# Retention on Trainium2: the product of values and decayed scores taken as three passes of rounded halves

## The reference

```python
def _retention(h, w_in, w_out):
    proj = h @ w_in
    q, k, v, g = jnp.split(proj, [RET_QK_W, 2 * RET_QK_W, 2 * RET_QK_W + RET_V_W], axis=-1)
    k = k * RET_QK_DIM ** -0.5
    ...
    def step(state, inp):
        q_i, k_i, v_i = inp
        scores = jnp.einsum('bhid,bhjd->bhij', q_i, k_i) * intra
        o = jnp.einsum('bhij,bhje->bhie', scores, v_i) \
            + jnp.einsum('bhid,bhde->bhie', q_i * q_dec, state)
        ...
    o = _rms_norm(o).reshape(B, L, RET_V_W).astype(h.dtype)
    y = jax.nn.silu(g) * o
    return y @ w_out
```

## Time and profile before

| | us |
|---|---|
| median of 3 runs | 1148.59 |
| lowest and highest run | 1146.23, 1149.07 |
| the profiled execution | 1149.55 |
| its span in the trace | 1147.7 |
| stretch of scores and products in it | 830.8 to 862.3 |

### The profile page before, as it was taken

One profiled execution on the slowest core, in us unless ns is written; L12 is line 12 of the kernel. 1 busy time (PEld: TensorE's weight loads), 2 busy tenths in 40 slices (PEclk: granted clock), 3 DMA queues, 4 the chain that ended last, 5 costly groups with the idle time before them and its releaser, 6 DMA issues.

```text
span 1147.7 us, 24128 instructions
## 1 busy us (share of the span) xinstructions
PE 1113.4 (97%) x8921; PEld 1061.7 (93%) x8921; DVE 777.3 (68%) x1404; ACT 624.1 (54%) x1194; POOL 338.4 (29%) x372
## 2 busy tenths in 40 slices
PE   6999999999989999999999999999999999999997
PEld 5976999999989888779999999999979999999996
DVE  5776489887478767737888554695456567887454
ACT  4656575556455656655656443474335555665443
POOL 3011414334301100126666321100023344665120
PEclk8999999999999999969999999999999999999998
DMA  6564337775556623214555545564513555555651
GB/s 197 131 178 146 92 107 208 193 199 164 188 173 194 211 74 111 75 37 148 182 158 173 184 161 197 198 194 156 170 48 111 187 179 184 183 183 190 205 180 48
DMA packets 202667, 180.63 MB, mean 157 GB/s; under 512 B 6849, under 2 KB 200804, under 8 KB 202468
## 3 DMA queue, kind: packets, MB, share of 16 engines
q1 hardware_dynamic: 201907, 175.74, 49.3%
q0 software_dynamic: 688, 3.94, 0.9%
HBM read 176.28 MB, written 1.05 MB: 155 GB/s over the span
## 4 chain that ended last, share of the span: by engine, by line
PE 86%; DVE 4%; ACT 4%; issue 2%; DMA 2%; POOL 1%; SPq 0%; ACTq 0%; DVEq 0%; POOLq 0%
PE ps L1942 25%; PE ps L1944 24%; PE ps L1943 24%; PE ps L2358 2%; DVE wlo L1314 2%; PE ps L2488 2%; PE ps L2100 1%; ACT whi L769 1%; POOL acc L590 1%; PE ps L2315 1%; DMA raw<-w_ffn_down 1%; PE ps L2340 1%; PE ps L2466 1%; DMA raw<-w_in 1%; PE ps L2314 1%
## 5 line engine op out<-in xcount | busy, mean ns | idle before, releaser
L1314 DVE TENSOR_TENSOR wlo<-raw,whi 128x1024 fp32r<-128x1024 f32 x316 | 395.9, 1289 | 155.4 <-ACT whi L769 153.7
L769 ACT ACTIVATE whi<-raw 128x1024 fp32r<-128x1024 f32 x316 | 318.4, 1051 | 164.2 <-PE ps L1944 142.1
L1942 PE MATMUL ps<-xh,whi 128*128 128x256 f32 (+1 forms) x880 | 250.7, 285 | 3.3 <-issue 2.1
L1943 PE MATMUL ps<-xl,whi 128*128 128x256 f32 (+1 forms) x880 | 248.4, 282 | 0.0
L1944 PE MATMUL ps<-xh,wlo 128*128 128x256 f32 (+1 forms) x880 | 248.2, 282 | 0.0
L1942 PE MATMUL ps<-xrh,whi 128*128 128x274 f32 (+2 forms) x832 | 241.8, 291 | 0.0
L1943 PE MATMUL ps<-xrl,whi 128*128 128x274 f32 (+2 forms) x832 | 238.3, 286 | 0.0
L1944 PE MATMUL ps<-xrh,wlo 128*128 128x274 f32 (+2 forms) x832 | 238.3, 286 | 0.0
L1944 PE MATMUL ps<-fh,wlo 128*128 128x256 f32 (+1 forms) x688 | 193.4, 281 | 0.0
L1943 PE MATMUL ps<-fl,whi 128*128 128x256 f32 (+1 forms) x688 | 193.3, 281 | 0.0
L1942 PE MATMUL ps<-fh,whi 128*128 128x256 f32 (+1 forms) x688 | 193.3, 281 | 0.0
(11 more groups left out here) (356 smaller groups left out, 1607.2 us busy)
## 6 DMA issues: line engine op xcount, KB each, us to landing
raw<-ffn_w SPq DMA_DIRECT2D x128, 512.0 KB, 4.4
raw<-ret_w_in SPq DMA_DIRECT2D x48, 512.0 KB, 4.4
raw<-even_w_in SPq DMA_DIRECT2D x24, 512.0 KB, 4.7
raw<-w_ffn_gate SPq DMA_DIRECT2D x22, 512.0 KB, 4.0
raw<-w_ffn_up SPq DMA_DIRECT2D x22, 512.0 KB, 5.2
raw<-w_ffn_down SPq DMA_DIRECT2D x16, 512.0 KB, 4.4
raw<-ret_w_out SPq DMA_DIRECT2D x16, 512.0 KB, 4.0
raw<-w_in SPq DMA_DIRECT2D x12, 512.0 KB, 5.6
```

Of the source, the lines that this page charges most:

```text
L769: A(whi[:, slot, s * 1024:s * 1024 + 1024], raw[:, slot, s * 1024:s * 1024 + 1024], ACT.Copy).then_inc(w_hi_ready, 1)
L1314: V.tensor_tensor(wlo[:, slot, s * 1024:s * 1024 + 1024], raw[:, slot, s * 1024:s * 1024 + 1024], f32(whi[:, slot, s * 1024:s * 1024 + 102 ...
L1942: T.matmul(dst, w[0], x[0], start=first, stop=False)
L1943: T.matmul(dst, w[0], x[1], start=False, stop=False)
```

## The change

The product of values and decayed scores is taken in three passes of rounded halves, by the helper `three`, in the place of one plain product. For this each operand needs a high and a low half:

- Values: ScalarE now copies the turned tiles from PSUM to `rv` with rounding (`value_high`, new), and VectorE subtracts `rv` from the same PSUM tiles to get the low halves (`ret_value_tiles`). They lie in space that is free at this time: `rv_far` where `xrh` is, and `rv_last` where `e` is.
- Scores: VectorE multiplies by `decay` as before, ScalarE rounds the result to `rsh` (`score_high`, new), and VectorE subtracts to get `rsl0` or `rsl1` (`ret_low`, new). `rsh` lies where `y` is, `rsl0` and `rsl1` in `ta` and `ra`.
- The products wait on the low halves (`rs_ready`), the scores on the product with `decay` (`rs_mul`, new).
- VectorE waits for all 16 tiles of `rqk` before the first low half of a value (`rqk_ready`, 16). This frees `xrh` and `e`.
- To have semaphores for this, four pairs of old ones are merged (`late_turned`, `lam_terms`, `cnorm_ready`), with counts adjusted.

```diff
-        rv = r1("rv", [P, 3, RH * RV])
+        rv = r1("rv", [P, 3, RH * RV], F32R)
...
+        rv_far = nc.alloc_sbuf_tensor_at("rv_far", [P, 2, RH * RV], F32R, offset=xr_at)
+        rv_last = nc.alloc_sbuf_tensor_at("rv_last", [P, RH * RV], F32R, offset=e_at)
+        rvl = [rv_far[:, 0, :], rv_far[:, 1, :], rv_last[:, :]]
+        rsh = nc.alloc_sbuf_tensor_at("rsh", [P, 2, 3, N2], F32R, offset=y_at)
+        rsl = [nc.alloc_sbuf_tensor_at("rsl0", [P, 3, N2], F32R, offset=ta_at), nc.alloc_sbuf_tensor_at("rsl1", [P, 3, N2], F32R, offset=ra_at)]
...
# ScalarE
+            def value_high(j, u):
+                act.wait_ge(vt_done, j + 1)
+                for t in range(3):
+                    n = TOK[t][1]
+                    ins = A(rv[0:n, t, at(256 * j, 256)], ps[4 + 2 * u + t // 2][0:n, 256 * (t % 2):256 * (t % 2) + 256], ACT.Copy)
+                    if t > 0:
+                        ins.then_inc(rv_hi, 1)
+            def score_high(hd):
+                for st in range(3):
+                    t0, sn = max(TOK[st][0], META), TOK[st][1]
+                    act.wait_ge(rs_mul, 3 * hd + st + 1)
+                    if st == 0 and hd >= 2:
+                        act.wait_ge(ro_done, 4 * (hd - 1))
+                    A(rsh[0:sn, hd % 2, st, t0:N2], rs[0:sn, hd % 2, st, t0:N2], ACT.Copy).then_inc(rs_hi, 1)
             def ret_chunks(i):
                 for u in range(2):
+                    if u == 1 or not is_first(i):
+                        value_high(2 * i + u - 1, 1 - u)
                     act.wait_ge(mm_done, E0["ret_v"] + 2 * i + u + 1)
...
             repeat(act, 4, ret_chunks)
+            score_high(0)
+            value_high(7, 1)
+            score_high(1)
...
-                if n % 4 == 2 and n >= 4:
-                    ret_rms(n // 4 - 1)
+                if q == 2 and hd >= 1:
+                    ret_rms(hd - 1)
+                if q == 3 and hd + 2 < RH:
+                    score_high(hd + 2)
# VectorE
             def ret_value_tiles(j, u):
-                dve.wait_ge(vt_done, j + 1)
                 for t in range(3):
                     n = TOK[t][1]
-                    V.tensor_copy(rv[0:n, t, at(256 * j, 256)], ps[4 + 2 * u + t // 2][0:n, 256 * (t % 2):256 * (t % 2) + 256]).then_inc(rv_ready, 1)
+                    dve.wait_ge(rv_hi, 2 * j + t // 2 + 1)
+                    V.tensor_tensor(rvl[t][0:n, at(256 * j, 256)], ps[4 + 2 * u + t // 2][0:n, 256 * (t % 2):256 * (t % 2) + 256],
+                                    f32(rv[0:n, t, at(256 * j, 256)]), ALU.subtract).then_inc(rv_ready, 1)
...
+            dve.wait_ge(rqk_ready, 16)
             repeat(dve, 3, ret_values)
...
+            def ret_low(hd):
+                for st in range(3):
+                    t0, sn = max(TOK[st][0], META), TOK[st][1]
+                    dve.wait_ge(rs_hi, 3 * hd + st + 1)
+                    V.tensor_tensor(rsl[hd % 2][0:sn, st, t0:N2], rs[0:sn, hd % 2, st, t0:N2], f32(rsh[0:sn, hd % 2, st, t0:N2]),
+                                    ALU.subtract).then_inc(rs_ready, 1)
...
             ret_decay(0)
             ret_value_tiles(7, 1)
+            ret_low(0)
             ret_decay(1)
+            ret_low(1)
             split_in("ret_v", 3, 2, 1)
...
                     ret_decay(hd + 2)
                 if hd >= 1:
                     ret_norm(hd - 1)
+                if hd + 2 < RH:
+                    ret_low(hd + 2)
# TensorE
-                    wait(pe, rs_ready, u - 1)
+                    wait(pe, rs_mul, u - 1)
...
-                        ins = T.matmul(ps[6 + n % 2][:, t0 - META:N1], rv[0:sn, st, RV * hd + P * q:RV * hd + P * q + P], rs[0:sn, hd % 2, st, t0:N2],
-                                       start=st == 0, stop=st == 2)
+                        v0 = RV * hd + P * q
+                        ins = three(ps[6 + n % 2][:, t0 - META:N1], (rv[0:sn, st, v0:v0 + P], rvl[st][0:sn, v0:v0 + P]),
+                                    (rsh[0:sn, hd % 2, st, t0:N2], rsl[hd % 2][0:sn, st, t0:N2]), st == 0, st == 2)
```

More of the change, by code:

```diff
@@ L185, in build @@
         y = sb("y", [P, KD, N2])
+        e_at = 32 * ((nc.sbuf_base + 31) // 32)
         e_mem = sb("e_mem", [P, KD * N1])
@@ L200, in build @@
         var = sb("var", [P, N2])
+        ta_at = 32 * ((nc.sbuf_base + 31) // 32)
         ta = sb("ta", [P, 2, N2])
@@ L203, in build @@
         b_col = sb("b_col", [P, 4])
+        ra_at = 32 * ((nc.sbuf_base + 31) // 32)
         ra = sb("ra", [P, 4, N2])
@@ L318, in build @@
         decay = r1("decay", [P, 4, 3, N2])
+        rv_far = nc.alloc_sbuf_tensor_at("rv_far", [P, 2, RH * RV], F32R, offset=xr_at)
+        assert 4 * 2 * RH * RV <= f1.at - xr_at
+        rv_last = nc.alloc_sbuf_tensor_at("rv_last", [P, RH * RV], F32R, offset=e_at)
+        assert RH * RV <= KD * N1
+        rvl = [rv_far[:, 0, :], rv_far[:, 1, :], rv_last[:, :]]
+        rsh = nc.alloc_sbuf_tensor_at("rsh", [P, 2, 3, N2], F32R, offset=y_at)
+        assert 4 * 2 * 3 * N2 <= e_at - y_at
+        rsl = [nc.alloc_sbuf_tensor_at("rsl0", [P, 3, N2], F32R, offset=ta_at), nc.alloc_sbuf_tensor_at("rsl1", [P, 3, N2], F32R, offset=ra_at)]
+        assert 4 * 3 * N2 <= 4 * 4 * N2
         r2 = Arena()
@@ L365, in build @@
         sel_ready, cum_ready, cum_hi, cum_lo = (sem(n) for n in ("sel_ready", "cum_ready", "cum_hi", "cum_lo"))
-        lam_sum, lam_exp, lam_one, lam_done = (sem(n) for n in ("lam_sum", "lam_exp", "lam_one", "lam_done"))
+        lam_terms, lam_exp, rs_mul, lam_done = (sem(n) for n in ("lam_terms", "lam_exp", "rs_mul", "lam_done"))
         oasq_ready, oastat, oarstd, oan, oa_hi, oa_lo = (sem(n) for n in ("oasq_ready", "oastat", "oarstd", "oan", "oa_hi", "oa_lo"))
@@ L609, in _ @@
             nc.gpsimd.tensor_tensor(acc2[:, 0:N1], acc2[:, 0:N1], sq6[:, 2, :], ALU.add).then_inc(conv_acc, 1)
-            pool.wait_ge(cmu_ready, 1)
+            pool.wait_ge(cnorm_ready, 1)
             for m in range(CT):
@@ L858, in _ @@
             squares(S_X, KD - 1, h[:, KD - 1, META:])
-            act.wait_ge(pt_done, 1)
+            act.wait_ge(late_turned, 2)
             A(ph[:, :, :], ps[6][:, :].rearrange("p (k n) -> p k n", k=2), ACT.Copy).then_inc(p_hi, 1)
             rms(S_X)
-            act.wait_ge(lam_sum, 2)
+            act.wait_ge(lam_terms, 2)
             A(lam_s[:, 2:4], lam_s[:, 0:2], ACT.Exp).then_inc(lam_exp, 1)
@@ L945, in _ @@
                     link(A(mu[:, 0:N1], ps[6][:, 0:N1], ACT.Copy, scale=1.0 / CONV_C))
-                    A(musq[:, 0:N1], mu[:, 0:N1], ACT.Square).then_inc(cmu_ready, 1)
+                    A(musq[:, 0:N1], mu[:, 0:N1], ACT.Square).then_inc(cnorm_ready, 1)
                 if i == CSTAT_AT + 3:
@@ L1384, in _ @@
                 V.tensor_tensor_reduce(var[0:1, 64 * j:64 * j + 64], lam_rows[:, 128 * j:128 * j + 64], lam_rows[:, 128 * j + 64:128 * j + 128],
-                                       1.0, 0.0, ALU.mult, ALU.add, lam_s[:, j:j + 1]).then_inc(lam_sum, 1)
-            dve.wait_ge(meta_done, 1)
+                                       1.0, 0.0, ALU.mult, ALU.add, lam_s[:, j:j + 1]).then_inc(lam_terms, 1)
+            dve.wait_ge(late_turned, 1)
             V.tensor_copy(h[:, :, 0:META], ps[5][:, 0:KD * META].rearrange("p (k n) -> p k n", k=KD)).then_inc(meta_ready, 1)
@@ L1519, in _ @@
                 if i == CSTAT_AT + 2:
-                    dve.wait_ge(cmu_ready, 1)
+                    dve.wait_ge(cnorm_ready, 1)
                     V.scalar_tensor_tensor(var[:, 0:N1], ps[6][:, N1:2 * N1], 1.0 / CONV_C, musq[:, 0:N1], ALU.mult, ALU.subtract).then_inc(cvar_ready, 1)
                 if i in (CSTAT_AT + 4, CSTAT_AT + 5):
-                    dve.wait_ge(crstd_ready, 1)
+                    dve.wait_ge(cnorm_ready, 2)
                     for m in ((0, 1), (2, 3))[i - CSTAT_AT - 4]:
@@ L1868, in ret_decay @@
                     dve.wait_ge(rs_done, u + 1)
-                    if st == 0 and hd >= 2:
-                        dve.wait_ge(ro_done, 4 * (hd - 1))
                     t0 = max(t0, META)
-                    V.tensor_tensor(rs[0:sn, hd % 2, st, t0:N2], ps[4 + u % 2][0:sn, t0:N2], decay[0:sn, hd, st, t0:N2], ALU.mult).then_inc(rs_ready, 1)
+                    V.tensor_tensor(rs[0:sn, hd % 2, st, t0:N2], ps[4 + u % 2][0:sn, t0:N2], decay[0:sn, hd, st, t0:N2], ALU.mult).then_inc(rs_mul, 1)
+            def ret_low(hd):
[4 more added lines that the diff above has]
+                                    ALU.subtract).then_inc(rs_ready, 1)
             def ret_norm(hd):
@@ L2044, in others @@
                     ins = T.transpose(ps[5][:, META * k:META * k + META], meta_rows[:, P * k:P * k + P], ident[0:META, 0:META])
-                ins.then_inc(meta_done, 1)
+                ins.then_inc(late_turned, 1)
                 pe.wait_ge(pos_in, 48)
@@ L2049, in others @@
                         ins = T.transpose(ps[6][:, N1 * kt + P * t:N1 * kt + P * t + P], pt[:, t, P * kt:P * kt + P], ident[:, :])
-                ins.then_inc(pt_done, 1)
```

(3 more changed lines are left out.)

8 lines of the change are left out of this document (4 added, 4 removed).

## The result

The changed kernel took 1155.4 us (median of 11 runs, 1153.07 to 1173.09), the kernel before 1147.16 us in the same hour (11 runs, 1144.93 to 1149.07). The ratio is 1.010 with a 95% interval of 1.0069 to 1.013, so it is slower: by 8.2 us in the medians, by 8 to 15 us in the interval. The forecast was 1154.1. The times of the changed kernel fall into two groups: six of the 11 runs lie between 1153.1 and 1155.4, five between 1163.4 and 1173.1; the kernel before has no such second group in any of 88 runs. What makes it is part of what follows. Every ratio in this document leaves out the runs that are over 1.5% above the fastest of their kernel (two of the changed kernel's, one of x4's and all five of x2's long ones), while the medians are over all runs.

What follows compares the result with a forecast made beforehand. TensorE was taken as the bound in both stages. Blocks 0, value stage 0, start +2.0, copy +0.7 and clock +2.8 sum to +5.5 us on the median 1148.59: 1154.1, range 1150.2 to 1159.5.

Steps and rivals of the forecast that it cites:

- Product blocks: Products of values and scores on TensorE: a block takes 1.33 us against 1.315, taken as 0 over 16 blocks.
- rival of short loads: Narrow passes of a block: rounded loads take half the time, a block 1.0 us, the kernel 1146.3; chance 0.08.
- dear narrow passes: Rival in the product blocks: narrow rounded passes cost like plain ones, a block 2.0 us, the kernel 1163; chance 0.04.
- ScalarE and VectorE in the value stage: While values are made: ScalarE's added copies and VectorE's subtractions fit into their idle time, cost 0.
- Start of the products: First products wait for a chain through ScalarE and VectorE, beginning at 837.55 instead of 835.53: +2.0 us.
- Copy of block 0: After blocks 0 and 1, TensorE waits 1.05 us for VectorE's late copy, where it waited some 0.3: +0.7 us.
- Clock: Product stage: TensorE's clock falls to 1.2 GHz between 837 and 841 us, returns with head 2's scores: +2.8 us.
- falls and comes back: Forecast case: the clock falls in the first product blocks and returns with head 2's dense scores, 1154.1; chance 0.53.
- stays down: Rival: the clock falls and stays low to the end of the product stage, +17 in all, 1165; chance 0.11.

Runs made afterwards that it cites:

- x4: The changed kernel with ScalarE's and VectorE's work at the start of the products reordered for a shorter wait; 1154.91 us, ratio 1.0075.
- x2: The kernel before with values and scores rounded and three passes of the same operands, no low halves or added wait; 1151.77 us, ratio 1.0009.
- x1: The changed kernel with one plain product of the high halves per product, low halves still made and waited for; 1154.47 us, ratio 1.0056.
- x3: The changed kernel with unread dense products in TensorE's waits, four ahead of the late score tile, two ahead of block 2; 1155.07 us, ratio 1.0058.
- x9: x3 with one more unread dense product ahead of each of the 8 blocks of heads 2 and 3; 1154.82 us, ratio 1.0057.
- x6: The changed kernel with the 64-token tile padded with zeros to 128 rows in its three passes; 1150.09 us, ratio 1.0014.
- x7: x2 with the 64-token tile padded with zeros to 128 rows; 1145.12 us, ratio 0.9967.
- x10: The changed kernel with both the start order of x4 and the padding of x6; 1145.61 us, ratio 0.9984.
- x11: The changed kernel run once more, unaltered; 1157.64 us, ratio 1.0085.
- x5: The kernel before, plain products kept, with the 64-token tile padded with zeros to 128 rows; 1144.65 us, ratio 0.9961.

## Why the prediction was right, and what in it was not

**Product blocks, 0.** Right: 1.31 us at the full clock where I had 1.33, and the account behind it (0.11 for an open load, 0.09 for a pause) was tested by padding: 1.05 us with rounded operands and 1.005 with plain ones, where it gives 1.0. The rival of short loads is wrong, and that of dear narrow passes too (2.0 a block). On the loads the trace shows nothing of the faster load that the Trainium skill has in TensorE: Matmul & The Clock Gate, section on fast weight load, if that is meant to hold for float32r. It fits another section of the same page, LDWEIGHTS, by which a load takes its columns divided by 1.2, whatever the rows: 128 columns make 107 ns, near the 0.11 seen here at the full clock with 64 and with 128 rows.

**ScalarE and VectorE in the value stage, 0.** Right: 43.00 of 43.00 us.

**Start of the products, +2.0.** Right: the wait is 1.89 us, and the first product comes 6.61 us after the first scores, where it was 4.72. The chain ran as described, link by link: this stage began 0.76 us earlier than the one that the prediction was drawn on, and with that added the first product is at 837.4 (forecast 837.55).

**Copy of block 0, +0.7.** Right in size, but not as a wait. In my sum the copy ended at 841.25, and two blocks at the low clock would fill the time up to it. On the same scale it ended at 841.1 (840.33 in the trace). Blocks 0 and 1 took 3.74 us together, just until it was done, and the old wait of 0.27 was gone: +0.84. That part was luck: I had both blocks at 1.86, and they were 1.44, in which the clock fell, and 2.30.

**Clock, +2.8.** The mechanism was right, fall and return (837.8 to 848.0), the size was not. The scores of head 2 cost +1.5, where I had 1.7, but blocks 2 and 3 cost +2.0, where I had 1.1. The mis-sized term is the block at the low clock: 1.86 in the prediction, 2.30 measured. There I let the streaming double and left a load at 0.11 us. The rows at 839.62 and 839.85 show two narrow passes, each paced by its load, 0.23 us apart: the load doubles as well. With the start the parts make +6.2, of 6.05 measured in the stage; the forecast was 5.5.

**The chances.** I treated "falls and comes back" and "stays down" as two worlds, one of which would be this kernel's. They are both its own: 10.2 us in one profiled execution and 51.2 in the other, and 8 of its 18 runs above 1160. I gave the second 0.11, at 1165; the runs in question lie at 1161 to 1173. The median hides this, and so did my range. That the median came out near the forecast is luck too: five of the 11 runs were long, and with a sixth it would have lain above 1160, outside my range.

**What makes the long stretch.** Of the kernels with rounded blocks, unpadded and unfilled (changed, repeated, x2, x4), 17 of 42 runs are above 1160. With plain blocks and the same wait (x1) it is 0 of 12, with fills (x3, x9) 0 of 14, with padding and rounded operands (x6, x7, x10) 0 of 36. Within one set the counts are 9 of 24 (x2, x4) against 0 of 20 (x1, x3), and 3 of 7 (x11) against 0 of 12 (x10) and 0 of 6 (x9); x6 and x7 had no unpadded rounded kernel beside them. So it is these blocks, not the waits. Why padding helps is not settled: it takes away the two pauses, and it also makes more rows busy and the stage shorter; the runs don't part these. Nor do they show what decides, within one kernel, which execution falls for long; the stage's beginning differs from run to run, and so does the moment at which the clock falls.

What also stays open: the lower group of the changed kernel is some 7.4 us above the kernel before (mean of the six runs 1154.6, against 1147.2), the stage of its profile only 6.05. The profiles cover one execution each, but the mean granted clocks on record show that low stretches differ between runs of every kernel. The kernel before took 1144.9 to 1147.2 us in its 18 runs at 0.982 or 0.983, and 1147.1 to 1153.2 in its 30 runs at 0.978 or less. In x9 the profiled run (1150.84, the clock held) and one more (1151.93) have 0.982 and 0.983, the other four (1154.1 to 1156.1) 0.979 or 0.980. So more time at the low clock goes with those 3 to 5 us; where in the kernel it lies, no profile shows.

## What to carry to other kernels

Before a product is swapped for more and thinner ones, count not its streaming but its loads, pauses and waits, and look at the granted clock of the nearest thin stretch: a wait of 1.9 us cost 1.6 by itself and 4.6 through the clock. Put other engines' work that TensorE doesn't need yet behind what it waits for next (here roundings and subtractions); the new order turned 1.9 us into 0.7, though it paid only together with the padding (x10 1145.61, x4 1154.91). And where a contraction of 64 rows stands between longer ones, try padding it with zeros: it gave 0.3 us a block in both forms of the product, and no padded kernel had a long low stretch. The three passes themselves gave nothing: with padding, the plain product has the lower time (x5 1144.65).
